# Weight sums of the down products: made ahead and parked in DRAM instead of made by GpSimd inside the down part

## The reference, cut to what matters

```
def conv_glu(hn, w_up, conv_f_w, conv_f_b, w_down):              # block 1
    up = hn @ w_up
    gate = gelu(causal_dwconv(up[..., :D_FF], conv_f_w, conv_f_b))
    return (gate * up[..., D_FF:]) @ w_down
...
y = (silu(u @ w_gate) * (u @ w_up)) @ w_down                     # block 2
```

## Time and profile before

| | us |
|---|---|
| median of three runs | 2802.05 |
| profiled execution | 2792.09 |
| its span | 2790.2 |
| PE busy | 2713.7 |
| DVE busy | 1776.0 |
| ACT busy | 1132.6 |
| POOL busy | 1406.1 |
| block 1, down part | 1115.13 to 1320.66 |
| block 2, up part (steady) | 2191 to 2514 |
| block 2, down part | 2533.72 to 2744.14 |

### The profile page before, as it was taken

The page is one execution under the profiler, slowest core; times in us unless marked ns, Lnnn a source line. Parts: engine busy times, 40 slices in busy tenths (PEclk is TensorE's granted clock), DMA queues, the critical chain, the costliest instruction groups (busy, mean ns, idle before and its releaser), DMA issues.

```text
span 2790.2 us, 36063 instructions
## 1 busy us (share of the span) xinstructions
PE 2713.7 (97%) x13022; PEld 2228.3 (80%) x13022; DVE 1776.0 (64%) x2041; ACT 1132.6 (41%) x1874; POOL 1406.1 (50%) x782
## 2 busy tenths in 40 slices
PE   8999999999999999999999999999998999998999
PEld 6888788888788888778887777778876888887876
DVE  7888642335966666987835446893359433338896
ACT  4256622242433333433414425553456333333434
POOL 4323212214699998732566331543254878876142
PEclk9999999999999999999999999999999999999999
DMA  4101222111122223240422110332023222224403
GB/s 152 38 23 39 99 92 90 38 44 62 62 75 90 82 75 137 97 136 33 156 92 91 46 39 24 135 117 80 23 92 127 83 90 74 84 90 151 151 1 136
DMA packets 84198, 233.51 MB, mean 84 GB/s; under 512 B 8432, under 2 KB 8688, under 8 KB 83312
## 3 DMA queue, kind: packets, MB, share of 16 engines
q1 hardware_dynamic: 73824, 199.06, 21.0%
q10 hardware_dynamic: 10256, 32.86, 3.2%
HBM read 193.62 MB, written 38.27 MB: 83 GB/s over the span
## 4 chain that ended last, share of the span: by engine, by line
PE 70%; issue 13%; DVE 9%; POOL 4%; ACT 2%; DMA 1%; ACTq 0%; SPq 0%; POOLq 0%; DVEq 0%
PE products L870 20%; PE others L1331 14%; PE products L1331 12%; PE products L1403 5%; PE others L1403 4%; POOL w_lo L672 2%; PE products L964 1%; PE others L870 1%; PE products L1266 1%; DVE w_lo L3216 1%; DMA w_raw<-wstream 1%; DVE act_lo L3211 1%; DVE work L2686 1%; PE products L993 1%; POOL w_hi L669 1%
## 5 line engine op out<-in xcount | busy, mean ns | idle before, releaser
L669 POOL TENSOR_TENSOR w_hi<-w_raw,small 128x1024 fp32r<-128x1024 f32 x54 | 110.3, 2043 | 586.9 <-PE products L870 329.8
L870 PE MATMUL products<-act_hi,w_hi 128*128 128x512 f32 x864 | 347.1, 402 | 1.5 <-DVE act_lo L2642 1.3
L870 PE MATMUL products<-act_lo,w_hi 128*128 128x512 f32 x864 | 338.4, 392 | 0.0
L728 POOL TENSOR_TENSOR w_lo<-w_raw,w_hi 128x512 fp32r<-128x512 f32 x200 | 305.9, 1534 | 64.3 <-ACT w_hi L2132 64.3
L870 PE MATMUL products<-act_hi,w_lo 128*128 128x512 f32 x864 | 338.1, 391 | 0.0
L672 POOL TENSOR_TENSOR w_lo<-w_raw,w_hi 128x1024 fp32r<-128x1024 f32 x94 | 251.5, 2675 | 144.0 <-ACT w_hi L2485 139.8
L870 PEld LDWEIGHTS products<-act_hi,w_hi 128*128 128x128 f32 x864 | 163.0, 189 | 42.4 <-issue 7.4
L2132 ACT ACTIVATE w_hi<-w_raw 128x512 fp32r<-128x512 f32 x240 | 146.1, 626 | 117.8 <-PE products L1331 51.2
L870 PEld LDWEIGHTS products<-act_hi,w_lo 128*128 128x128 f32 x864 | 163.0, 189 | 34.7
L870 PEld LDWEIGHTS products<-act_lo,w_hi 128*128 128x128 f32 x864 | 163.3, 189 | 31.2
L964 PE MATMUL products<-act_hi,w_hi 128*128 128x512 f32 x408 | 166.0, 407 | 8.5 <-DVE act_lo L3671 4.9
(11 more groups left out here) (619 smaller groups left out, 7268.4 us busy)
## 6 DMA issues: line engine op xcount, KB each, us to landing
w_raw<-wstream SPq DMA_DIRECT2D x155, 512.0 KB, 3.4
w_raw<-wstream SPq DMA_DIRECT2D x168, 256.0 KB, 2.6
parked_hidden<-work SPq DMA_DIRECT2D x40, 512.0 KB, 3.0
raw<-wstream SPq DMA_DIRECT2D x28, 512.0 KB, 7.5
raw<-parked_hidden SPq DMA_DIRECT2D x20, 512.0 KB, 6.6
work<-parked_hidden SPq DMA_DIRECT2D x20, 512.0 KB, 7.6
work<-xT ACTq DMA_DIRECT2D x16, 512.0 KB, 8.9
work<-wstream SPq DMA_DIRECT2D x12, 512.0 KB, 6.0
```

Of the source, the lines that this page charges most:

```text
L669: pool.tensor_tensor(w_hi[:, slot, :], w_raw[:, slot, :], zeros, ALU.add)\
L728: pool.tensor_tensor(ring_lo[slot], part_source[(n - 1) % 7], ring_hi[slot].bitcast(F32), ALU.subtract)\
L870: last = pe.matmul(out[:, c], a[:, ws, w], x[:, k, c], start=(k == 0 and i == 0), stop=(k == KT - 1 and i == 2))
```

## The change

The four sums of each of the ten pairs of blocks are made before the down part and kept in a DRAM tensor, `parked_sums` (10 pairs of two tiles of 512 KB). The down part loads them like weights: after steps 0 and 1 have used A11 and A12, `down_upper` is overwritten by the tile with A11-A21 and A21+A22; `down_lower` gets the tile with the other two sums in place of A21 and A22; A22 (the corner) is loaded by itself, 256 KB in pieces of 512 bytes.

In block 1 POOL makes the sums in W[18..19] between the splits of q1, attention and xo1: counting blocks from 0, sums 0, 1 and 2 behind the splits of q1's blocks 2, 4 and 6, sums 3 to 7 behind the split of xo1's block 1, sums 8 and 9 behind those of xo1's blocks 2 and 4. SP loads each pair of blocks when the pair before is stored, and stores the result when the four sums are done.

In block 2 DVE makes them in W[0..1], one pair of blocks per chunk, in the pair j = 1: two operations between `hidden` and `up_second`, two between `gate_second` and `up_first`. SP stores them in the next chunk's first pair, ahead of that pair's last fetch, and then loads the next two blocks. The tenth store follows the load of the lower tiles; step 0 waits for it.

POOL has no sums left in either down part. Two semaphores get new names and counts.

```
+                def park_sums(c):                                # SP, block 2
+                    sp.wait_ge(s("factor_made"), of.weight_sum(c, 0))
+                    sp.dma_start(parked_sums[c + (-1)].rearrange("n p t -> p n t"), sums_at[name]).then_inc(s("parked_moved"), 16)
...
                     else:
                         store_hidden(c + (-1), 1)
+                        if name == "ffn2":
+                            park_sums(c + (-1))
                     sp.wait_ge(s("parts_split"), of.split(c, 7 * j + 7))
                     fetch(3, at + up)
+                    if name == "ffn2" and not j:
+                        sp.wait_ge(s("parked_moved"), of.sums_stored(c + (-2)))
+                        move_block(c)
...
                 for i in range(1, ROUND):
                     down_tiles_lower(i, 0)
+                if name == "ffn2":
+                    park_sums(BLOCKED)
...
+                for r in range(ROUNDS):
+                    u0 = STEP_UNITS * r
                     for i in range(ROUND):
+                        sp.wait_ge(s("factor_lo"), of.factor_low(u0 + ROUND + i))
+                        down_sums(i, r)
...
                     for i in range(ROUND):
+                        sp.wait_ge(s("factor_lo"), of.factor_low(u0 + 2 * ROUND + i))
+                        down_corner(i, r)
+                    if r + 1 < ROUNDS:
+                        for i in range(ROUND):
+                            sp.wait_ge(s("factor_lo"), of.factor_low(u0 + 4 * ROUND + i))
+                            hidden_tiles(i, r + 1, 0)
+                            down_tiles(i, r + 1)
+                        for i in range(ROUND):
+                            sp.wait_ge(s("factor_lo"), of.factor_low(u0 + 6 * ROUND + i))
+                            hidden_tiles(i, r + 1, 1)
+                            down_tiles_lower(i, r + 1)
...
+            for b in range(q0 + 3, f1):                          # SP, block 1
+                at = b - q0
+                if at == 3:
+                    move_block(0)
+                sp.wait_ge(s("weights_split"), b - 1)
+                load(b, b % 2)
+                if at in (4, 6, 8):
+                    park_sums((at - 4) // 2)
+                elif at in (5, 7, 9):
+                    move_block((at - 3) // 2)
+                elif at == 11:
+                    for n in range(3, 8):
+                        park_sums(n)
+                        move_block(n + 1)
...
-            split_blocks(BLOCK0["q1"] + 2, BLOCK0["ffn1"] + 4)
+            def weight_sums(n):                                  # POOL, block 1
+                up_, low_ = (lambda k: sum_block("ffn1", 0, k)), (lambda k: sum_block("ffn1", 1, k))
+                pool.wait_ge(s("block_moved"), 32 * (n + 1))
+                pool.tensor_tensor(low_(1), low_(0), low_(1), ALU.add).then_inc(s("parts_summed"), 1)
+                pool.tensor_tensor(low_(0), up_(0), low_(0), ALU.subtract).then_inc(s("parts_summed"), 1)
+                pool.wait_ge(s("parts_summed"), 4 * n + 1)
+                pool.tensor_tensor(up_(0), low_(1), up_(0), ALU.subtract).then_inc(s("parts_summed"), 1)
+                pool.wait_ge(s("parts_summed"), 4 * n + 3)
+                pool.tensor_tensor(up_(1), up_(1), up_(0), ALU.subtract).then_inc(s("parts_summed"), 1)
+            for b in range(q0 + 2, BLOCK0["ffn1"] + 4):
+                split(b, b // 2, b % 2)
+                for n in {2: (0,), 4: (1,), 6: (2,), 9: range(3, 8), 10: (8,), 12: (9,)}.get(b - q0, ()):
+                    weight_sums(n)
...
-                for r in range(ROUNDS):                          # POOL, down part
-                    for i in range(ROUND):
-                        down_sum(0, r, i)
-                        down_sum(1, r, i)
-                    for i in range(ROUND):
-                        down_sum(2, r, i)
-                    for i in range(ROUND):
-                        down_sum(3, r, i)
...
                     hidden(*before)                              # DVE, up part
+                    if j and not conv_tiles:
+                        weight_sums(c, False)
                     up_second(c, j)
                     gate_second(c, j)
+                    if j and not conv_tiles:
+                        weight_sums(c, True)
                     up_first(c, j)
...
                     elif not conv_tiles:                         # DVE, step_added
-                        dve.wait_ge(s("mem_in"), 144)
+                        dve.wait_ge(s("parked_moved"), of.sums_stored(BLOCKED - 1))
```

More of the change, by code:

```diff
@@ L186, in summed, with weight_sum, blocks_moved, sums_stored @@
         return c * 8 + (self.first_summed - 8 + n)
-    def down_summed(self, n):
-        return self.first_summed + 8 * BLOCKED + n
+    def weight_sum(self, c, n):
+        return c * 4 + (self.first_weight_sum + n)
+    def blocks_moved(self, c):
+        return c * 32 + 16 * self.sums_moved
+    def sums_stored(self, c):
+        return c * 16 + 16 * (self.sums_parked + 1)
     def loaded(self, c, unit):
@@ L206, in factor_made @@
     def factor_made(self, n):
-        return self.factors_made + 16 + n
+        return self.first_weight_sum + self.weight_sums + n
 def unit_of(u):
@@ L218 @@
 FACTOR_SUM_AT = {(_n, _r, _i): _at + 1 for _at, (_u, _n, _r, _i) in enumerate(FACTOR_SUMS)}
[L221 to L227, removed]
+TILE_SEM = {(_kind, _i): _k for _i in range(5) for _kind, _k in (("first", _i), ("sums", _i), ("second", 5 + (_i > 1)), ("lower", 7), ("corner", 7))}
+TILES_OF = [3, 3, 3, 3, 3, 2, 3, 10]
+TILES_LATER = {"first": 1, "sums": 0, "second": 0, "lower": 5, "corner": 0}
 def tile_loaded(ffn, kind, i, r):
     k = TILE_SEM[kind, i]
-    return k, 32 + 16 * TILES_OF[k] * (ROUNDS * ffn + r + 1) + 16 * ffn
+    return k, 32 + 16 * (TILES_OF[k] * (ROUNDS * ffn + r + 1) - TILES_LATER[kind]) + 16 * ffn
 def x_loaded(k, n):
@@ L631, in _, with move_block, park_sums @@
             reordered(2, 18)
-            loads(18, f1 - f1 % 2)
-            reordered(f1 - f1 % 2, f1)
+            def move_block(n):
+                if n:
+                    sp.wait_ge(s("parked_moved"), Seven("ffn1").sums_stored(n - 1))
+                else:
+                    sp.wait_ge(s("product_quarters"), 4 * BLOCK0["q1"])
+                for m in range(2):
+                    sp.dma_start(W[:, 18 + m, :], ap["wstream"][f1 + 6 * n + 4 + m]).then_inc(s("block_moved"), 16)
+            def park_sums(n):
+                sp.wait_ge(s("parts_summed"), 4 * n + 4)
+                sp.dma_start(parked_sums[n].rearrange("m p t -> p m t"), sums_at["ffn1"]).then_inc(s("parked_moved"), 16)
+            q0 = BLOCK0["q1"]
+            loads(18, q0 + 3)
+            for b in range(q0 + 3, f1):
[12 more added lines that the diff above has]
+                        move_block(n + 1)
+                elif at == 12:
+                    park_sums(8)
+                elif at == 13:
+                    move_block(9)
+                elif at == 14:
+                    park_sums(9)
             parts("ffn1")
@@ L754, in chunk @@
                         low(c, n + 7)
[L756 to L779, removed]
                 def down_low(u):
@@ L2174, in down_high @@
                     r, s_, i = unit_of(u)
[L2175 to L2178, removed]
-                        act.wait_ge(s("parts_summed"), of.down_summed(down_sum_at((0, 0, 1, 2, 0, 3)[s_], r, i)))
+                    kind = ("first", "first", "lower", "sums", "sums", "lower", "corner")[s_]
+                    k, count = tile_loaded(AT_FFN[name], kind, i, r)
+                    act.wait_ge(s(f"x_in{k}"), count)
                     act.activation(by_o(down_hi[slot]), down_source(name, s_, i), ACT.Copy).then_inc(s("parts_high"), 1)
@@ L2474, in _ @@
             act.wait_ge(s("sw_o_lo"), 5)
-            load(W[:, 16, :], parked_scale, "scale_moved")
+            load(W[:, 16, :], parked_scale, "parked_moved")
             half_out("out2", 4)
@@ L3288, in ffn @@
                 up_second(BLOCKED, 1)
+                if not conv_tiles:
+                    weight_sums(BLOCKED, False)
                 gate_second(BLOCKED, 1)
+                if not conv_tiles:
+                    weight_sums(BLOCKED, True)
                 factor_low(1)
@@ L3521, in _ @@
                 if n == 18:
[L3522 removed]
+                    dve.wait_ge(s("block_moved"), 32 * BLOCKED + 64)
                 z2_out(n)
```

79 lines of the change are left out of this document (53 added, 26 removed).

## The result

The changed kernel took 2762.1 us (median of 4 runs, 2759.5 to 2764.2) where the kernel before took 2800.2 in the same comparison; the ratio is 0.986 [0.985, 0.988]. A second comparison gave 2764.2 (4 runs) against 2797.8 (23 runs), ratio 0.9885 [0.9865, 0.9905]. The forecast of 2772.5 had the right sign and mechanism and was 8 to 10 us too careful; the lower end of its range, 2763, lies 0.9 us above the first measured median.

The account below looks back on a forecast made before the run. Bound: DVE slowed by POOL's 20 sums at each down-part round's start. 35.1 us gone, 3.9 + 0.5 + 1 + 0.2 back, so 29.5 off the 2802.05 median: 2772.5 us; likeliest case 2765 to 2780, 8 in 10 2763 to 2789.

Parts of the forecast that it names:

- What bounded the kernel, and its removal: Down parts: DVE slowed by POOL's 20 sums at each round's start; without them PE bounds both rounds, -15.1 and -20.0 us.
- The base and the term that go with it: Whole kernel: 29.5 us gain taken from the three-run median 2802.05, not from the profiled 2792.1, giving 2772.5.
- 35.1 gone: Both down parts: PE's loss of 15.1 and 20.0 us against 190.4 us of matmuls each, all removed.
- The 9.10 us operation of the earlier trace: Down parts: one POOL sum stretched to 9.10 us under back-to-back DVE work, cited for DVE and POOL slowing each other.
- The new wait in block 2: Down part, unit 7: DVE's step 0 waits for the tenth store, landing at 2553.3; cost 3.9 us, bounds 0 and 7.
- Block 1's sums: POOL beside q1, attention, xo1: rounds of 14.4 us, sums 7 end at 598.3; attention costs 0.5 us, bounds 0 and 3.
- Rival (a): Block 1's one buffer: sums 7 end after 607.9, PE waits in xo1, slower beyond rounds of 24.2 us; chance 0.05.
- Block 2's up part: DVE's sums and SP's store there nearly hidden: 1 us over ten chunks, bounds 0 and 20.
- two narrow margins: Block 2's up part: only 0.4 us to spare on both POOL's low beside DVE's sums and the fetch behind SP's store.
- Rival (b): Block 2's up part: slacks fail, PE stands 0.8 us in each of 20 pairs, 16 us back, 2787.5; chance 0.18.
- (c): Down parts: DVE stays slow without POOL, or tiles come late and gaps return as DMA waits, 2802; chance 0.05.
- Costs in all: Given back: 3.9 new wait, 0.5 attention, 1 up part, 0.2 late lows; 5.6 us in all.

Follow-up runs that it names:

- early_park: Changed kernel with block 2's store of the tenth pair of sums issued ahead of lower tiles 1 to 4 instead of behind them: 2758.6 us.

## Why the prediction was right in kind and wrong in size

- *What bounded the kernel, and its removal.* Right, and shown from both sides by taking the sums out and putting idle ones in. The down parts went from the 205.53 and 210.42 us that were read to 190.50 and 196.72, so all of the 35.1 us but the new gap.
- *The base and the term that go with it.* This step failed: the term "35.1 gone" together with "It lies 10 us under the median of the three runs, so I take the difference from the median." The 10 us were read as a constant beside the change. They were 4.6 us by which the first three runs lay above the median of 58 (2802.05 against 2797.4), which is the luck of three runs, and 5.3 by which the profiled execution lay below it. The latter are in the very term that was removed: its down parts were 6.2 and 6.4 us shorter than in the other two profiled executions, everything else 1.7 and 2.9 longer. On medians the term is 2797.4 - 2755.6 = 41.8 us, not 35.1; the other two profiles give 41.3 and 41.4. So 2772.5 becomes 2772.5 - 4.65 - 6.7 = 2761.2, and 1.7 for costs that were set too low gives 2762.9, the median of all eight runs of the changed kernel. The 9.10 us operation of the earlier trace rows was quoted as a sign of contention; that DVE kept its pace beside it, so that the same code had a second, faster way to run, was missed.
- *The new wait in block 2.* Place and mechanism right; taken at 3.9, measured 6.2 (196.7 - 190.5), within the bounds of 0 and 7. The landing was put at 19.6 us into the part and came at 20.2; the clock cost 2.3, not 1.2. That transfer was counted as data at a rate, behind lower tiles that had to land first; early_park shows a store that takes 14 us from issue, with those tiles ahead of it or behind it. So the working was wrong, and that the landing came within 0.6 us of it is luck. (Its 2.3 us for 1 MB would take 456 GB/s; the trace that was read shows 422 at most over 2 us there.)
- *Block 1's sums.* Round 14.4 forecast, 14.9 measured; the end of sums 7, 598.3 against 598.6, the closer for a q1 that began 2.8 us earlier than in the trace that was read; attention 0 instead of 0.5. Rival (a) needed rounds of 16.8 us before PE would wait at all.
- *Block 2's up part.* 1 us forecast, 0.7 and 1.2 seen, and of its two narrow margins only the fetch's gave way. Rival (b) did not occur, nor (c).
- *Costs in all.* 5.6 forecast, 2762.9 - 2755.6 = 7.3 measured, good to about 2 us with 8 and 5 runs: the traces give 6.2 for the gap and about 1 for the up part.

## What to carry to other kernels

Where one profiled execution stands off the timed median, profile it again before pricing the stall, and ask whether the stage that the change removes is the one that scatters (in this case a POOL instruction stretched to many times its length was a mark of it): if so, the difference belongs to the term and not to the base. Idle work that nobody waits for separates contention from dependency in one run. A store that an in-order engine will wait for is issued ahead of the bulk: what that gained here is the 6 us by which it was issued earlier, not a faster landing.

## What the runs showed of the hardware that I had not expected

- DVE and POOL on SBUF have two ways of meeting. Either they alternate, and 512-column operations go from 0.60 to a pitch of 1.69 us on DVE and to 1.6 to 1.7 on POOL; or DVE keeps its pitch of 0.60 and one POOL operation hangs until DVE's run of operations that read both inputs from SBUF is over (17 cases, 3 to 11.4 us). The Trainium skill (SBUF — State Buffer, Who interferes with whom) calls the shared port pair an exclusive lock. Alternation agrees with it. If it is such a lock, the hanging operation shows that one given back every 0.6 us need not go to the engine that waits: POOL got nothing at 13 DVE operations in a row.
- Ten POOL operations a round cost 27.6 us in the four rounds when they came back to back beside a DVE that needs 2.4 of every 2.72 us, and ten of the same size 3.9 when they fell later in the round, where most came one to a unit and some back to back behind one that hung. All twenty cost 36.7, more than the 31.5 of both together.
- A 1 MB store issued while the DMA engines were full (397 GB/s over 17 us) landed after 12.5 to 14.1 us in all eight kernels that make it (the changed one and its seven versions), whether four tiles of 512 KB were issued ahead of it or behind it. The same store in attention took 4.0 (DMA issues of the changed kernel from 538 to 600 us: count, KB each, us to landing):

```profile
parked_sums<-work SPq DMA_DIRECT2D x5, 1024.0 KB, 4.0
```
